# Four FFN products among the projection's last turns, half the stored tiles deferred in the merge, and a projection that opens with two tiles

## The chip, the cores and the metric

The kernel runs on one core of one Trainium2 chip. A core has TensorE (PE: matmuls, with a weight load of its own, PEld), VectorE (DVE), ScalarE (ACT), GpSimd (POOL), SyncE (SP) and 16 DMA engines that all queues share. Matmuls write to PSUM, eight banks of 512 fp32 columns for each partition. The metric is the device time of one execution in microseconds; less is better.

## The reference

One step of a hybrid backbone on 128 context and 1024 latent tokens, width 1024, fp32. Three token mixers (mLSTM, HGRN2, attention) give branches of width 512. What matters here is what follows them:

```
branches = jnp.stack([y_ml, y_hg, y_at], axis=2)
proj_b = jnp.einsum('blnw,nwd->blnd', branches, p['w_branch'])
gates_b = jax.nn.sigmoid(bg.reshape(B, L, N_BRANCH, D_MODEL))
merged = jnp.sum(gates_b * proj_b, axis=2)
x = x + g1 * (merged @ p['w_out'])

h2 = _rmsnorm(x, p['norm2_g']) * (1 + sc2) + sh2
gu = h2 @ p['w_ffn_in']
gt, up = gu[..., :FFN_HIDDEN], gu[..., FFN_HIDDEN:]
x = x + g2 * ((jax.nn.silu(gt) * up) @ p['w_ffn_out'])
```

FFN_HIDDEN is 2816, and a last RMSNorm gives the outputs.

## The kernel before

Every fp32 operand of a matmul is split in two parts (hi by ACT, a copy to fp32r; lo by DVE, the difference), and a product is three passes, hi*hi, hi*lo and lo*hi (`three_passes`, L59). Features lie on partitions and the 1152 tokens are columns (T = 1152, three groups of TH = 384), except where rows of tokens are needed. Each engine runs its own program, in the order written, and they meet by counting semaphores: `x.then_inc(s, 1)` on one, `wait_ge(s, n)` on another. Phases end with a barrier of all engines (L77 to L79).

**Merge** (`blend`, first half). For each of 8 tiles t of 128 output features, the sigmoid of three gate tiles multiplies three branch products, and the sum goes to `merged[:, t]`. The product of branch 0 was made earlier and lies in DRAM ("stored", `b0_dram`); branch 1 (operand `ys`, n=1) and branch 2 (operand `wide` in `zb`, n=2) are made here by `branch_tile`, 36 matmuls of 384 columns to three banks, 0 to 2 for even tiles and 3 to 5 for odd ones. The product n=1, t=0 is already in its banks when the phase begins. For n=1, DVE multiplies the stored tile by its gate into `merged` (L2300), takes the product out of PSUM times its gate to `part` (L2303) and adds it (L2307); for n=2 it does the last two (L2303, L2309). `taken` counts the operations that use up a gate, and PE starts a tile when the tile two before it has been taken. POOL issues the loads of gate tiles to a ring of four buffers (L2185), each when an older gate is used; SP issues stored tiles to two buffers (L2140), the parts of branch 2 (L2144), its weights (L2147) and w_out in eight parts (L2166). ACT makes the sigmoids (L2215). Between tiles ACT and DVE split branch 2 (L2275), its weights (L2279) and w_out (L2206, L2283), and at the end `merged` itself (`merged_hi` L2211, `merged_lo` L2289, which writes over the gate buffers).

**Projection** (`blend`, second half), nine tiles i of 128 tokens. PE: 48 matmuls of 512 columns, banks 2(i%2) and the next; then `turn(i-1)`, eight transposes (L2390). DVE: `residual` (times g1, L2336, count `gated`; plus x, L2340), `modulated` (two operations on the turned tile, L2348, L2351) and `split` (L2355). ACT: the store of x1 to DRAM (L2244), a square with sum (L2247), a scaling (L2251) and the hi part of the FFN's input (L2255). POOL: mean and power -0.5 (L2188, L2190). The FFN's first weight is split at the end (L2263, L2366).

**FFN** (`ffn`). 22 steps of 128 hidden features. In a step PE makes six products of 24 matmuls of 384 columns (gate for three token groups, then up), and puts 18 output products of the step before among them; step 0 has none and stands ahead of the loop. ACT makes silu (L2497), DVE multiplies by up (L2591), both split the result (L2501, L2596), and DVE adds each output product to `acc` (L2569), which takes the memory of `merged` and is loaded with x1 from DRAM (L2456).

## Time and profile before

| | us |
|---|---|
| median of 3 runs | 2532.36 |
| lowest, highest | 2531.53, 2533.96 |
| the profiled execution | 2528.88 |
| its span, first to last instruction | 2527.0 |
| merge, from the barrier ahead of it to PE's last product | 1449.97 to 1551.97 |
| projection, from PE's first matmul to its last turn | 1557.26 to 1673.45 |
| FFN, from PE's first matmul | 1682.52 on |

The span is what the rows add up to; the rest of an execution's time lies around it. The mean granted clock of TensorE is 0.985 of full speed; its two levels are 1.2 and 2.4 GHz (0.50 and 1.00). A row of the timeline gives the start, the busy time, the engine and line, and in brackets how long the engine stood idle before it and what released it. "issue" as a releaser means that the profile shows none. A stretch gives, for each engine, its busy time and its number of instructions, then the granted clock, the mean busy share of the DMA engines and what they moved.

### The profile page before, as it was taken

How to read it: one execution, taken by the hardware profiler on the slowest of the kernel's cores; microseconds unless marked ns; L12 is line 12 of the kernel's file. 1: busy time of each engine (PE TensorE's matmuls, PEld its weight loads, DVE VectorE, ACT ScalarE, POOL GpSimd, SP SyncE). 2: the span in 40 equal slices, each digit the busy share in tenths (PEclk: the TensorE clock that was granted, in tenths of full speed). 3: DMA queues.
4: the chain of work that ended last, by engine and by line, in shares of the span. 5: the costliest groups of instructions: out<-in, count | busy, mean ns of one | idle time of the engine just before them, and what ended most of it. 6: DMA issues, size and time to landing. Idle time of an engine off the chain costs nothing. (4 is left out here: it accounts for less than half of the span.)

```text
span 2527.0 us, 41706 instructions
## 1 busy us (share of the span) xinstructions
PE 2432.8 (96%) x17387; PEld 2240.3 (89%) x17387; DVE 1187.3 (47%) x1773; ACT 678.1 (27%) x1036; POOL 155.7 (6%) x194
## 2 busy tenths in 40 slices
PE   6999999999999999989999999979999999999998
PEld 4887789999999899888999898869999999999997
DVE  3331111003543667645555476445555555555555
ACT  3321111113332232234444453232112112112112
POOL 0000000001100011112111010110000000000000
PEclk8999999999999999999999999989999999999999
DMA  6224532225453333142002093231011011011012
GB/s 264 107 84 175 196 121 82 97 70 186 165 176 115 134 116 113 56 131 74 17 17 83 19 388 107 99 142 42 33 50 41 33 50 41 33 50 41 33 50 84
DMA packets 98125, 247.19 MB, mean 98 GB/s; under 512 B 12593, under 2 KB 56065, under 8 KB 88657
## 3 DMA queue, kind: packets, MB, share of 16 engines
q1 hardware_dynamic: 61200, 174.69, 20.0%
q10 hardware_dynamic: 32832, 55.46, 5.9%
q0 software_dynamic: 3968, 15.21, 1.6%
q8 instruction: 99, 1.62, 0.3%
q14 instruction: 26, 0.21, 0.0%
HBM read 183.85 MB, written 61.55 MB: 97 GB/s over the span
## 5 line engine op out<-in xcount | busy, mean ns | idle before, releaser
L59 PE MATMUL ps<-zb,wt 128*128 128x384 f32 x2400 | 651.5, 337 | 10.4 <-DVEq L2617 9.1
L59 PEld LDWEIGHTS ps<-zb,wt 128*128 128x128 f32 x2400 | 441.6, 188 | 28.4 <-DVEq L2617 9.5
L2569 DVE TENSOR_TENSOR merged<-merged,ps 128x512 f32<-128x512 f32 x378 | 259.5, 687 | 322.7 <-PE ps L59 320.1
L59 PE MATMUL ps<-xb,wt 128*128 128x384 f32 x1056 | 358.5, 340 | 0.0
L59 PE MATMUL ps<-ys 128*128 128x512 f32 x1056 | 298.2, 394 | 0.0
L59 PE MATMUL ps<-h_hi,fill_whi 128*128 128x384 f32 x672 | 234.7, 349 | 7.0 <-PEq L79 3.6
L59 PE MATMUL ps<-h_hi,fill_wlo 128*128 128x384 f32 x672 | 225.8, 336 | 0.0
L59 PE MATMUL ps<-h_lo,fill_whi 128*128 128x384 f32 x672 | 225.6, 336 | 0.0
L59 PEld LDWEIGHTS ps<-xb,wt 128*128 128x128 f32 x1056 | 198.5, 188 | 17.3
L59 PEld LDWEIGHTS ps<-ys 128*128 128x128 f32 x1056 | 193.3, 188 | 16.6
L59 PE MATMUL ps<-prj_whi,h_hi 128*128 128x512 f32 (+1 forms) x432 | 164.9, 382 | 6.1 <-DVE h_lo L553 6.1
L59 PE MATMUL ps<-prj_wlo,h_hi 128*128 128x512 f32 (+1 forms) x432 | 162.5, 376 | 0.0
L59 PE MATMUL ps<-prj_whi,h_lo 128*128 128x512 f32 (+1 forms) x432 | 162.3, 376 | 0.0
L1758 PEld LDWEIGHTS ps<-att_va,att_pt 128*128 128x128 f32 x1152 | 145.4, 191 | 6.6
L1758 PE MATMUL ps<-att_va,att_pt 128*128 128x65 f32 x1152 | 144.1, 270 | 0.0
L2501 ACT ACTIVATE ys<-zf 128x384 fp32r<-128x384 f32 x66 | 34.7, 526 | 395.8 <-DVE zf L2591 395.8
L538 DVE TENSOR_TENSOR prj_wlo<-prj_raw,prj_whi 128x2048 fp32r<-128x2048 f32 (+1 forms) x20 | 43.5, 2189 | 194.2 <-ACT prj_whi L454 193.9
L59 PEld LDWEIGHTS ps<-h_hi,fill_whi 128*128 128x128 f32 x672 | 126.6, 188 | 7.1 <-issue 4.2
L59 PEld LDWEIGHTS ps<-h_lo,fill_whi 128*128 128x128 f32 x672 | 127.0, 189 | 3.0 <-issue 3.0
L59 PE MATMUL ps<-h_hi,prj_whi 128*128 128x384 f32 x384 | 128.3, 334 | 0.8 <-ACT prj_tst L472 0.8
L59 PE MATMUL ps<-h_lo,prj_whi 128*128 128x384 f32 x384 | 128.3, 334 | 0.0
L59 PE MATMUL ps<-h_hi,prj_wlo 128*128 128x384 f32 x384 | 128.3, 334 | 0.0
(348 smaller groups left out, 3708.3 us busy)
## 6 DMA issues: line engine op xcount, KB each, us to landing
wraw<-in_w_ffn_in SPq DMA_DIRECT2D x22, 1024.0 KB, 4.8
prj_raw<-in_w_ada SPq DMA_DIRECT2D x16, 1024.0 KB, 5.9
fill_raw<-in_w_fill SPq DMA_DIRECT2D x30, 512.0 KB, 4.2
bg_dram<-fill_st ACTq DMA_DIRECT2D x72, 192.0 KB, 2.0
xf<-bg_dram POOLq DMA_DIRECT2D x24, 576.0 KB, 7.9
tok_dram<-prj_tst ACTq DMA_DIRECT2D x45, 256.0 KB, 2.1
zf<-in_w_ffn_out SPq DMA_DIRECT2D x22, 512.0 KB, 3.5
prj_raw<-in_w_tok SPq DMA_DIRECT2D x10, 1024.0 KB, 6.5
```

Source lines behind the costliest of these rows:

```text
L59: mm = pe.matmul(out, lhs[a], rhs[b], start=first and n == 0, stop=last and n == 2)
L538: v.tensor_tensor(w[1][b % 2][:, at], raw[u % NR][:, 0:width], w[0][b % 2][:, at].bitcast(F32), ALU.subtract).then_inc(lo_done, 1)
L1758: mm = pe.matmul(ps[:, OB, a * H1:a * H1 + H1], pt[j % 3][:, a * P:a * P + P], va[:, j, kv, :], start=False, stop=j == NT - 1 and a == G - 1)
L2501: act.activation(a[0][s][:, t * TH:t * TH + TH], gate[:, t * TH:t * TH + TH], ACT.Copy).then_inc(a_hi, 1)
L2569: v.tensor_tensor(dst, dst, ps[:, bank, :], ALU.add).then_inc(added, 1)
```

## The change

In the merge:

- The third tile (n=1, t=2) is written to banks 6, 7 and 2, and its first two thirds wait for nothing.
- Of the eight stored tiles, 4 to 7 are used in the second branch: their multiplication and addition stand ahead of the product of n=2, t=4 to 7. In n=1 these tiles have neither, and the product goes straight to `merged`. The order of the gate loads (`GATES`) follows, and `place` gives the count of each. SP loads both weights before stored tiles 4 and 5, and 6 and 7 after w_out.
- The first `merged_lo` stands between the last product and its addition. PE opens the projection when n=2, t=6 has been taken.

In the projection:

- Tiles 0 and 1 are multiplied together, part by part of the inner dimension.
- Turns lag by two tiles. Each x tile is loaded into the buffer where x1 is made, when the x1 of two tiles before has been stored and scaled, and DVE writes the product to `xs` first. The odd turned tiles go to `hole`.
- The FFN's first weight is split around tiles 2 and 3 into the free end of `merged` (`g.first_w`). After turn 7 PE makes the gate products of token groups 0 and 1, then turn 8, then their up products.

In the FFN: banks (2, 3, 6) for gate, (0, 1, 7) for up, 4 and 5 for output. PE makes only the third group of step 0, gate and up. ACT and DVE do the work of step 0 in a new order. SP waits for these two products before it loads the second half of x1, whose place `first_w` takes, and with it before the loop's loads.

```diff
@@ blend @@
+        APART = (6, 7, 2)
+        GATES = [(n, t) for t in range(4) for n in range(2)] + [(1, t) for t in range(4, 8)]
+        GATES += [(2, t) for t in range(4)] + [(n, t) for t in range(4, 8) for n in (0, 2)]
+        place = {x: i for i, x in enumerate(GATES)}
...
             for i in range(2, NT):
-                sp.wait_ge(x1_done, i - 1)
-                sp.dma_start(xin[i % 2], io["x_sample"][i * P - P:i * P, :]).then_inc(x_in[i % 2], 16)
+                sp.wait_ge(x_out[i % 2], 16 * (i // 2))
+                sp.wait_ge(xs_done, i - 1)
+                sp.dma_start(x1[i % 2], io["x_sample"][i * P - P:i * P, :]).then_inc(x_in[i % 2], 16)
...
+                        if n == 1:
+                            v.tensor_tensor(into, done[t % 2], bg[at % 4], ALU.mult).then_inc(taken, 1)
+                        else:
+                            link(v.tensor_tensor(done[t % 2], done[t % 2], bg[at % 4], ALU.mult))
+                            v.tensor_tensor(into, into, done[t % 2], ALU.add).then_inc(taken, 1)
...
+                    if n == 2 and t == 7:
+                        merged_lo(0)
...
+                if m == 2:
+                    branch_tile(pe, ps, t, [x[s] for x in w], ys[n], APART, range(2))
+                    pe.wait_ge(taken, place[1, 0] + 1)
+                    branch_tile(pe, ps, t, [x[s] for x in w], ys[n], APART, range(2, 3)).then_inc(mm_done, 1)
+                    continue
...
+            pe.wait_ge(taken, place[2, 6] + 1)
+            for k in range(KD):
+                pe.wait_ge(m_lo, k + 1)
+                pe.wait_ge(wo_lo, k + 1)
+                out(0, k)
+                if k == 0:
+                    pe.wait_ge(taken, 8 * NB)
+                out(1, k)
+            for i in range(2, NT):
+                pe.wait_ge(gated, i - 1)
+                for k in range(KD):
+                    out(i, k)
+                turn(i - 2)
...
+            turn(NT - 2)
+            pe.wait_ge(next_lo, 1)
+            pe.wait_ge(gated, NT - 1)
+            for t in range(2):
+                pe.wait_ge(h_lo, 3 * t + 3)
+                first(0, t)
             turn(NT - 1)
+            pe.wait_ge(gated, NT)
+            for t in range(2):
+                first(1, t)
@@ ffn @@
+            for n in range(2):
+                if n:
+                    sp.wait_ge(gu_mm, 6)
+                sp.dma_start(g.acc[:, 1 + 4 * n:5 + 4 * n, :],
+                             g.x1_dram[P + 4 * n * P:5 * P + 4 * n * P, :].rearrange("(t p) d -> p t d", p=P)).then_inc(x1_in[n], 16)
...
-            step(0, 0, first=True)
+            pe.sem_inc(gu_mm, 4)
+            for up in range(2):
+                for k in range(KD):
+                    mm = three_passes(pe, ps[:, (UP if up else GATE)[2], 0:TH], [x[:, k, up * P:up * P + P] for x in g.first_w],
+                                      [x[:, k, 2 * TH:3 * TH] for x in g.h], k == 0, k == KD - 1)
+                mm.then_inc(gu_mm, 1)
```

PE at the start of the merge, with the waits on `taken` (its semaphore is listed under the name of its first owner, prj_sig_done). Before:

```order
L59 MATMUL ps<-ys,wt 128x384 x36
L59 MATMUL ps<-ys,wt 128x384 [waits prj_sig_done]
L59 MATMUL ps<-ys,wt 128x384 x35
L59 MATMUL ps<-ys,wt 128x384 [waits prj_sig_done]
L59 MATMUL ps<-ys,wt 128x384 x35
```

The same place in the changed kernel:

```order
L59 MATMUL ps<-ys,wt 128x384 x60
L59 MATMUL ps<-ys,wt 128x384 [waits prj_sig_done]
L59 MATMUL ps<-ys,wt 128x384 x11
L59 MATMUL ps<-ys,wt 128x384 [waits prj_sig_done]
L59 MATMUL ps<-ys,wt 128x384 x35
```

The first wait now stands behind 60 matmuls instead of 36.

DVE at the end of the merge, n=2, from the product of t=6. In the kernel before L2303 is a product, L2309 its addition, L2283 a split of w_out and L2289 one of merged:

```order
L2303 TENSOR_TENSOR xf<-ps,xf 128x1152
L2309 TENSOR_TENSOR merged<-merged,xf 128x1152
L2283 TENSOR_TENSOR wt<-wraw,wt 128x1024
L2303 TENSOR_TENSOR xf<-ps,xf 128x1152
L2309 TENSOR_TENSOR merged<-merged,xf 128x1152
L2283 TENSOR_TENSOR wt<-wraw,wt 128x1024
L2289 TENSOR_TENSOR xb<-merged,zb 128x1152 x2
```

And in the changed one, where these are L2319, L2326, L2289 and L2295, and L2310 and L2311 use a stored tile:

```order
L2319 TENSOR_TENSOR xf<-ps,xf 128x1152
L2326 TENSOR_TENSOR merged<-merged,xf 128x1152
L2289 TENSOR_TENSOR wt<-wraw,wt 128x1024
L2310 TENSOR_TENSOR xf<-xf 128x1152
L2311 TENSOR_TENSOR merged<-merged,xf 128x1152
L2319 TENSOR_TENSOR xf<-ps,xf 128x1152
L2295 TENSOR_TENSOR xb<-merged,zb 128x1152
L2326 TENSOR_TENSOR merged<-merged,xf 128x1152
L2295 TENSOR_TENSOR xb<-merged,zb 128x1152
```

Two operations on the stored tile now stand ahead of the last product, and the first split of merged right behind it.

PE at the end of the projection, from the last matmul of tile 8. Before:

```order
L59 MATMUL ps<-wt,xb 128x512
L2390 MATMUL ps<-ident,merged 128x128 [waits prj_t_ev,prj_blk_done]
L2390 MATMUL ps<-ident,merged 128x128 x7
L2390 MATMUL ps<-ident,merged 128x128 [waits prj_t_ev,prj_blk_done]
L2390 MATMUL ps<-ident,merged 128x128 x7
L77 UNCONDITIONAL_BRANCH
L2677 UNCONDITIONAL_BRANCH [waits barrier_Pool_Activation_PE_DVE_SP_release]
L59 MATMUL ps<-zb,wt 128x384 [waits prj_rstd_done,fill_hi]
```

In the changed kernel (`mergedr` is the memory of `merged` under another type, here `first_w`):

```order
L59 MATMUL ps<-wt,xb 128x512
L2411 MATMUL ps<-ident,merged 128x128 [waits prj_t_ev,prj_blk_done]
L2411 MATMUL ps<-ident,merged 128x128 x7
L2411 MATMUL ps<-ident,merged 128x128 [waits prj_t_ev,prj_blk_done]
L2411 MATMUL ps<-ident,merged 128x128 x7
L59 MATMUL ps<-zb,mergedr 128x384 [waits prj_t_out0,prj_h_split,prj_t_out3]
L59 MATMUL ps<-xb,mergedr 128x384
L59 MATMUL ps<-zb,mergedr 128x384 x2
```

The two turns behind tile 8 are now 6 and 7, and FFN products follow them; turn 8 comes after 48 such matmuls and is followed by 48 more.

## Rows read from the trace of the kernel before

**Rows 1.** The page: busy time of PE and its share of the span.

```profile
PE 2432.8 (96%) x17387; PEld 2240.3 (89%) x17387; DVE 1187.3 (47%) x1773; ACT 678.1 (27%) x1036; POOL 155.7 (6%) x194
```

**Rows 2.** Waits of PE, 1440 to 1750 us: total, times, longest.

```profile
PE ps L59 <- DVEq L2617: 9.1, 1, 9.1
PE ps L2390 <- ACT merged L2251: 6.8, 1, 6.8
PE ps L59 <- issue: 6.7, 2, 5.3
PE ps L59 <- DVE xf L2303: 4.1, 1, 4.1
```

**Rows 3.** Stretches: length, busy time by engine, clock, DMA share, GB/s.

```profile
828.60:833.50 4.90, 4.87 (x128) 4.53 (x128) 0.34 (x2) 0.49 (x1) 0.00 (x0) 1.00 1.14 290
809.40:813.40 4.00, 4.00 (x14) 4.00 (x15) 1.21 (x1) 0.49 (x1) 0.58 (x2) 0.57 0.75 233
...
1456.46:1460.52 4.06, 0.00 (x0) 0.00 (x0) 2.73 (x3) 3.46 (x3) 0.54 (x1) 0.75 1.03 375
1460.52:1465.30 4.78, 4.78 (x15) 4.78 (x16) 4.71 (x4) 1.25 (x2) 1.56 (x3) 0.50 0.93 364
1465.30:1500.44 35.14, 35.14 (x203) 34.82 (x201) 27.18 (x21) 18.82 (x16) 5.46 (x11) 1.00 1.02 413
1502.00:1550.00 48.00, 48.00 (x278) 48.00 (x278) 30.89 (x23) 16.76 (x16) 3.24 (x6) 1.00 0.51 170
...
1557.26:1560.90 3.64, 3.64 (x9) 2.86 (x10) 3.64 (x4) 3.64 (x4) 0.00 (x0) 0.50 0.00 0
...
1581.90:1592.90 11.00, 11.00 (x51) 9.05 (x50) 4.23 (x4) 3.25 (x4) 1.32 (x2) 1.00 0.33 105
...
1673.45:1682.52 9.07, 0.00 (x0) 0.00 (x0) 6.06 (x5) 1.91 (x3) 0.28 (x1) 0.50 0.00 0
1682.52:1687.20 4.68, 4.68 (x15) 4.68 (x16) 0.00 (x0) 3.07 (x2) 0.71 (x2) 0.50 0.67 211
```

**Rows 4.** Timeline of DVE in the merge: the products of n=1, t=1, 2 and 3.

```profile
1463.17 1.35 DVE L2303 TENSOR_TENSOR xf<-ps,xf 128x1152 f32<-128x1152 f32 x1
...
1469.35 1.36 DVE L2303 TENSOR_TENSOR xf<-ps,xf 128x1152 f32<-128x1152 f32 x1 [1.47 <-PE ps L59]
...
1476.67 1.36 DVE L2303 TENSOR_TENSOR xf<-ps,xf 128x1152 f32<-128x1152 f32 x1 [1.51 <-ACT xf L2215]
```

**Rows 5.** Timeline of PE: three gaps and what released it.

```profile
809.38 0.41 PE L59 MATMUL ps<-h_hi,fill_whi 128*128 128x384 f32 x1 [2.11 <-PEq L79]
...
828.63 0.34 PE L59 MATMUL ps<-h_hi,fill_whi 128*128 128x384 f32 x1 [2.84 <-issue]
...
1449.97 6.49 PE L59 MATMUL ps<-ys,wt 128*128 128x384 f32 x36 [1.27 <-PEq L79]
```

**Rows 6.** Timeline of DVE at the end of the merge.

```profile
1552.01 1.36 DVE L2303 TENSOR_TENSOR xf<-ps,xf 128x1152 f32<-128x1152 f32 x1 [2.36 <-PE ps L59]
1553.40 1.36 DVE L2309 TENSOR_TENSOR merged<-merged,xf 128x1152 f32<-128x1152 f32 x1
1554.68 1.22 DVE L2283 TENSOR_TENSOR wt<-wraw,wt 128x1024 fp32r<-128x1024 f32 x1
1555.81 2.62 DVE L2289 TENSOR_TENSOR xb<-merged,zb 128x1152 fp32r<-128x1152 f32 x2
```

**Rows 7.** Timeline: residual of tile 8 on DVE, and its turn on PE.

```profile
1663.83 1.23 DVE L2336 TENSOR_TENSOR merged<-ps,zf 128x1024 f32<-128x1024 f32 x1 [5.78 <-PE ps L59]
...
1671.48 1.97 PE L2390 MATMUL ps<-ident,merged 128*128 128x128 f32 x8 [6.82 <-ACT merged L2251]
```

**Rows 8.** FFN opening: ACT's and DVE's weight splits; a load, us to landing.

```profile
1682.39 1.91 ACT L2491 ACTIVATE wt<-wraw 128x2048 fp32r<-128x2048 f32 x1 [2.41 <-SPq L2451]
...
1688.61 2.29 DVE L2563 TENSOR_TENSOR wt<-wraw,wt 128x2048 fp32r<-128x2048 f32 x1 [7.37 <-DMA hole<-gate_rows]
...
wraw<-in_w_ffn_in SPq DMA_DIRECT2D x1, 1024.0 KB, 11.4
```

More of the change, by code:

```diff
@@ L2081, in _, with branch_tile @@
             tile(7, False, False)
-def branch_tile(pe, ps, t, ws, y):
+def branch_tile(pe, ps, t, ws, y, banks=None, thirds=range(3)):
     ws = [x.rearrange("p (k n) -> p k n", k=4) for x in ws]
-    for c in range(3):
+    banks = banks or [3 * (t % 2) + c for c in range(3)]
+    for c in thirds:
         for k in range(4):
-            mm = three_passes(pe, ps[:, 3 * (t % 2) + c, 0:TH], [x[:, k, t % 4 * P:t % 4 * P + P] for x in ws],
+            mm = three_passes(pe, ps[:, banks[c], 0:TH], [x[:, k, t % 4 * P:t % 4 * P + P] for x in ws],
                               [y[:, 4 * b + k, c * TH:(c + 1) * TH] for b in range(2)], k == 0, k == 3)
     return mm
+GATE, UP, OUT = (2, 3, 6), (0, 1, 7), 4
 def blend(nc, g):
@@ L2260, in _ @@
                     split(i - 1)
-            act.wait_ge(ahead, 32)
-            act.wait_ge(o_mm, NT)
-            act.activation(g.wt[:, 0, :], raw[0], ACT.Copy).then_inc(next_hi, 1)
+                if i == 2:
+                    act.wait_ge(ahead, 32)
+                    act.activation(flat(g.first_w[0]), raw[0], ACT.Copy).then_inc(next_hi, 1)
             split(NT - 1)
@@ L2496, in gated @@
                     act.wait_ge(a_lo, 3 * j + t - 2)
-                act.activation(gate[:, t * TH:t * TH + TH], ps[:, GATE + t, 0:TH], ACT.Silu).then_inc(silu, 1)
+                act.activation(gate[:, t * TH:t * TH + TH], ps[:, GATE[t], 0:TH], ACT.Silu).then_inc(silu, 1)
             def a_split(j, s, t):
@@ L2528, in _ @@
             act.sem_inc(w_hi, 1)
-            step(0, 0, first=True)
+            w_split(1, 1, True)
+            for t in range(2):
+                gated(0, t, FIRST[0][t], True)
+            prompt_hi(0, 0, pw[0], True)
+            out_hi(0, 0, True)
+            a_split(0, 0, 0)
+            a_split(0, 0, 1)
+            gated(0, 2, FIRST[0][2], True)
+            a_split(0, 0, 2)
             with act.Fori(0, NH // 2 - 1) as i:
@@ L2596, in a_split, with step @@
                 v.tensor_tensor(a[1][s][:, r], gate[:, r], a[0][s][:, r].bitcast(F32), ALU.subtract).then_inc(a_lo, 1)
-            def step(j, s, first=False):
-                if not first:
-                    adds(j - 1, range(0, 3))
-                w_split(j + 1, 1 - s, first)
-                if not first:
-                    adds(j - 1, range(3, 6))
+            def step(j, s):
+                adds(j - 1, range(0, 3))
+                w_split(j + 1, 1 - s)
+                adds(j - 1, range(3, 6))
                 prompt_lo(j, s, pw[0], pw[1])
-                if not first:
-                    adds(j - 1, range(6, 9))
+                adds(j - 1, range(6, 9))
                 out_lo(j, s)
@@ L2609, in step @@
                     u = 9 + 3 * t
-                    if not first:
-                        adds(j - 1, range(u, u + 2))
+                    adds(j - 1, range(u, u + 2))
                     times_up(j, t, 3 + t)
-                    if not first:
-                        adds(j - 1, range(u + 2, u + 3))
+                    adds(j - 1, range(u + 2, u + 3))
                     a_split(j, s, t)
             v.sem_inc(w_lo, 1)
+            w_split(1, 1, True)
+            times_up(0, 0, FIRST[1][0])
+            times_up(0, 1, FIRST[1][1])
             v.wait_ge(g2_in, 32)
-            step(0, 0, first=True)
+            prompt_lo(0, 0, pw[0], pw[1])
+            out_lo(0, 0)
+            a_split(0, 0, 0)
+            a_split(0, 0, 1)
+            times_up(0, 2, FIRST[1][2])
+            a_split(0, 0, 2)
             v.wait_ge(cleared, 1)
-            v.wait_ge(x1_in, 32)
+            v.wait_ge(x1_in[0], 16)
             with v.Fori(0, NH // 2 - 1) as i:
@@ L2693, in group, with step @@
             def group(j, s, up, t, k):
[L2694 removed]
+                return three_passes(pe, ps[:, (UP if up else GATE)[t], 0:TH], [x[s][:, k, up * P:up * P + P] for x in w],
                                     [x[:, k, t * TH:t * TH + TH] for x in g.h], k == 0, k == KD - 1)
[L2697 removed]
+            def step(j, s):
                 pe.wait_ge(w_lo, j + 1)
@@ L2705, in step @@
                             mm.then_inc(gu_mm, 1)
-                        if k in (2, 5, 7) and not first:
+                        if k in (2, 5, 7):
                             u = 3 * n + (2, 5, 7).index(k)
                             out(j - 1, 1 - s, range(u, u + 1))
-            step(0, 0, first=True)
+            pe.sem_inc(gu_mm, 4)
[4 more added lines that the diff above has]
+                mm.then_inc(gu_mm, 1)
             with pe.Fori(0, NH // 2 - 1) as i:
@@ L2798, in build @@
         attention(nc, g)
-        g.merged = sb("merged", [P, KD, T])
+        with nc.sbuf_tensor("merged", [P, KD, T], F32) as g.merged:
+            pass
+        g.mergedr = sb("mergedr", [P, KD * T], F32R)
         with nc.sbuf_tensor("xf", [P, KD, T], F32) as g.xf:
```

124 lines of the change are left out of this document (59 added, 65 removed).

## Prediction

> **What bounds the kernel now.** I read the page first, then who waited for whom on TensorE (PE) between 1440 and 1750 us, then the stretches around each wait with their granted clock, then the rows of the engine that released PE. PE is busy for 96% of the span [rows 1], and no other engine is near that, so only two things can be won: time in which PE stands still, and time in which it works at its lower clock. Before the FFN's loop there are five standstills in the stages that the change touches [rows 2]: 4.07 us at the merge's third tile, 1.36 and 5.29 us (together the 6.7 of "issue", at 1500.44 and 1551.97), 6.82 us before the last turn and 9.07 us before the FFN. Behind three of them the clock is at half: 4.78 us at 0.50, 3.64 us at 0.50 and 4.68 us at 0.50 [rows 3]. All the rest of these 270 us is full-speed PE work, which the change neither adds nor removes: the same 144 products of the FFN's first step, the same 9 tiles, the same turns. The units are 35.14 us for 203 records, 0.173 us for a matmul of 384 columns (6.25 us for a merge tile of 36, 4.2 us for one FFN product of 24), and 11.00 us for a projection tile of 48; a turn adds 0.8 [rows 3].
>
> **The merge's opening.** Before, the third tile (t=2) starts at 1460.52, after VectorE (DVE) has taken the first tile out of its banks. After, two thirds of it (24 matmuls, 4.2 us) go to banks 6 and 7 and need no wait, so they run from 1456.3 to 1460.5; the last third then needs what is ready at 1460.5 anyway. PE reaches t=3 at 1462.6. That tile wants t=1 taken, which DVE ends at 1463.17 + 1.35 = 1464.5 [rows 4]: 1.9 us of new wait. t=3 ends at 1470.8. t=4 wants t=2 taken: 1469.35 + 1.36, now in two instructions, about 1470.9, no wait. It ends at 1477.1, and t=5 wants t=3 taken, at 1476.67 + 1.36 = 1478.0, because that product waited for its gate [rows 4]: 0.9 us. The gates of t=4 to 7 come one for each 6.25 us of PE instead of two; on the saturated queues (1.02 of the 16 engines, 413 GB/s, [rows 3]) they came some 2.9 us apart, so they are no bound. t=7 ends at 1484.3 + 2 x 6.25 = 1496.9, against 1500.44. The 1.36 us behind it also goes: DVE no longer makes the stored product and the addition in t=6 and can split the first weight half by 1494.3, since both weights are now loaded ahead of the deferred tiles. **Term A: 1501.81 - 1496.9 = 4.9 us.** Half of that is the half clock after the 4.07 us wait: 216 matmuls take 39.9 us before and 37.5 at full clock.
>
> **The merge's second half** has the deferred work: for t=4 to 7 DVE does four operations of 1.36 us instead of two, plus a split of 1.22 in two of the tiles, 6.7 us against PE's 6.25. Two of the four need no product of that tile and run while DVE waited before (it idled 2.36 us ahead of t=7 [rows 6]). Counted from t=3 with starts 1.28 us apart where nothing depends and 1.40 where it does, DVE reaches the last product 0.6 us after PE has ended it. PE itself is never held, since it needs a tile taken only two tiles later. **Term B, the seam to the projection.** Before: product 1.36, addition, one w_out split, then the first part of merged's lower half, which ends at 1557.2, and PE starts: 5.29 us [rows 6]. After: 0.6 late, product, then the lower half at once: 0.6 + 1.28 + 1.36 + 0.1 = 3.3 us. The gain is **2.0 us**. From there PE needs a new part only for each 12 matmuls (2.7 us) instead of each 6, and DVE delivers one every 1.3 to 2.6, so two tiles interleaved don't starve. The price of the clock behind this gap: 0 to 2.3 us. A gap of 2.84 us left it at 1.00, one of 2.11 us was followed by 4.00 us at a mean of 0.57, one of 4.06 us by half clock [rows 3, 5]. 3.3 lies nearer the last, so I take 1.8 (3.64 us at half clock costs 1.8, [rows 3]), as much as before, plus 0.3 us gained on the small waits inside the first tile. The Trainium skill ("TensorE: Matmul & The Clock Gate", What's actually happening) says that the number of matmuls at the low clock differs between runs of the same kernel; the rows above, where 2.11 us cost more than 2.84, agree, and by it this term is a draw of lots and not a rule of gap length.
>
> **Term C, the last turn.** Turns now lag by two tiles, and the residual of tile i waits for turn i-2. At the end PE does tile 8, turns 6 and 7 (1.6 us), then two FFN gate products (8.4), and only then turn 8. Counting from the end of tile 8, DVE first modulates tile 6 and splits tile 5 (0.9 to 4.6), then starts the residual of tile 8. From there to the turn it took 1671.48 - 1663.83 = 7.65 us before, by way of ScalarE's (ACT) square, GpSimd's power and ACT's scaling [rows 7]. So turn 8 can start at 12.25, and PE gets there at 10.0: a wait of 2.25 instead of 6.82, **4.6 us gained**. The products' own inputs are in time: split 5 at 4.6 against the second product at 5.8.
>
> **Term D, the barrier.** After turn 8 PE has two more products, 8.4 us, to 21.4. DVE does modulation 7, split 6, split 7 (ACT is free for it at 12.2), modulation 8 (needs turn 8, starts 14.5) and split 8, done at 19.3. So PE itself is last at the barrier, and the gap is what it was at the barrier ahead of the merge, which PE reached last as well, 1.27 us [rows 5], instead of 9.07: **7.8 us**. The weight split of 2.29 us has moved to tile 3, where DVE has 4 us to spare per tile. **Term E, the clock.** With no long gap there, the 4.68 us at half clock behind the barrier give 2.3 back, and the turn that took 1.97 us takes 0.8: **3.4 us** with rounding.
>
> **Term F, what is new in the FFN's opening.** PE has only two products (8.4 us) after the barrier before the second step, where before it had six (25 us). After 9 matmuls more, at 10.1, the first output product wants the first activation split (a_lo). The chain to that, from ACT's start [rows 8]: ACT's split 1.91, DVE's 2.29, but then the gate rows, which landed only at 1688.6, that is at 6.2; from there the lower half of 1024 columns at DVE's 1.23 us for as many [rows 7], two multiplications of 512 with the gate rows to 8.8, ACT's 1024 columns at 1.0 (half of its 1.91 for 2048), DVE's 1.23, and 0.6 for the 384 columns of the activation: 11.7. **Cost 1.6 us.** Before, this chain had 17 us of cover. A second one: SyncE now waits for those two products before it loads the second half of x1 (2 MB) and, behind that in its queue, the weight of step 2. DVE's split of that weight is queued ahead of its additions, and PE's sixth output product at 22.9 wants those. At 413 GB/s 3 MB take 7.6 us; landing at 17.5 to 18.5, then 1.9 + 2.3 + 0.7, gives 22.4 to 23.4: **0.3 us**. Another 0.1 for the third projection tile, which now waits for DVE to take the first.
>
> **The sum.** 4.9 + 2.0 + 0.3 + 4.6 + 7.8 + 3.4 - 1.6 - 0.3 - 0.1 = **21.0 us**. The profiled execution took 2528.9 us (span 2527.0), so the same one would be 2507.9. The median of the runs is 3.5 us higher, 2532.4, so I forecast 2511.4 us, 0.8% less. The bank numbers in the FFN's loop, the semaphore more and the buffer of the odd tiles cost nothing, because the loop is bound by PE and DVE idles beside it.
>
> **Rivals.**
> 1. The clock falls otherwise. If it stays up at the seam, 1.8 us less: 2509.6. If it also falls at one of the small waits (1.9, 2.25, 1.27, 1.6 us), 1.7 to 3.4 more: 2513 to 2515. For: the 2.11 us case [rows 5]. Against: the 1.36 us ahead of 1501.81 had 1.00 on both sides [rows 3].
> 2. The weight of step 2 comes late. For: the weight asked for at 1691 took 11.4 us to land behind the x1 loads [rows 8]. Landing at 21.4 instead of 18 costs 3.4 us: 2515. Against: 2 MB stood ahead of it then that are through now. The Trainium skill ("DMA: Bandwidth & Descriptors", Queues, rings and completion order) has each DMA engine take turns between its queues, a packet at a time; both loads are on one queue, so by that they come one after the other, as in my count.
> 3. The merge's second half is bound by DVE or by the gates, two of which are now needed per tile and are asked for only when older ones are used. If each of the last three tiles loses 1 to 1.5 us, 3 to 4.5 us: 2514 to 2516. Against: the second half moved 170 GB/s at 0.51 of the DMA engines [rows 3], and the four deferred tiles and gates add 4.7 MB, less than 100 GB/s, to it.
> 4. The change does not cover what it should: turn 7 stands ahead of the first FFN product, and its tile's chain ends at 12.25 after tile 7, while PE arrives at 12.6. If ACT or GpSimd is 3 us late there, the wait just moves ahead of the products, and the last turn's with it: up to 4 us, 2515.
> 5. Slower. The low clock, once there, holds on through the small waits: over the two seam tiles (20 us more) and from the end of tile 8 to the FFN's second step (29.2 us of full-speed work, less 3.9 of waits that it hides). That is 45 us more: 2557. It decides from 21 us of added time at half clock on. For: half clock held through the whole 9.07 us wait and 4.68 us beyond [rows 3]. Against: in the rows it was back after 3.6 to 4.8 us of work each time, and no gap over 3.3 us is left.
>
> **Chances.** Forecast (2509.5 to 2513) 0.60; clock stays up 0.10, falls again 0.08; late weight 0.08; second half 0.06; uncovered turn 0.03; no net gain 0.03; slower 0.02. A measurement of this kernel tells about 0.2%, 5 us, from no change, so faster 0.95, same 0.03, slower 0.02. The range takes in rivals 1 to 4 and one microsecond of spread of the median: 2506 to 2518.
>
> **What would show it.** PE's waits before the FFN's loop should read about 1.9, 0.9, 3.3, 2.3, 1.3 and 1.6 us. The second branch starts near 1496.9, the projection near 1550.4, and the clock is full from the projection's second tile on. The chain's last barrier is released by PE and not by DVE. Wrong would be: a wait of DVE for a stored tile or a gate beyond t=4, a wait at the first FFN products, half clock behind the barrier, or any PE wait inside the FFN's loop.

## The result and the profile after

| | before | after |
|---|---|---|
| median, us | 2532.82 (2531.53 to 2533.96, 4 runs) | 2512.17 (2509.91 to 2516.67, 4 runs) |
| ratio to before, 95% interval | | 0.9919, 0.9907 to 0.9931 |
| profiled execution, and its span | 2528.88, 2527.0 | 2512.39, 2510.5 |

The change takes 20.7 us off the median (by the interval 17.5 to 23.6). The forecast of 2511.4 us for the median was 0.8 us too low. The sum behind it, 2507.9 us for the profiled execution, was 4.5 us too low, and where these 4.5 us are is what most of the rest is about. All tables here count from S, PE's first matmul of the merge. The program ahead of S is the same in all kernels, but S lies anywhere from 1448.6 to 1456.2 us in the fourteen traces. In after it lies 1.4 us earlier than in before, so from S to the end the sum missed by 5.9 us and not by 4.5. Three executions of 4843, 5822 and 8446 us (one of before, two of `both_ends_again`), far outside all others, are left out of the ratios and of that kernel's median.

| us | merge, S to PE's last product | from there to PE's first matmul behind the FFN's barrier | from there to the end | S to the end |
|---|---|---|---|---|
| before | 102.0 | 130.6 | 844.5 | 1077.0 |
| forecast | 97.1 | 131.7 | 827.3 | 1056.0 |
| after | 97.2 | 132.6 | 832.1 | 1061.9 |
| the same kernel again | 96.0 | 131.6 | 831.8 | 1059.4 |

The forecast's row is that of before with the terms of the sum taken off, and 16.8 us (four products) moved from the third column into the second. The first two columns are right within 1.1 us. The third is 4.5 to 4.8 us off.

The page of after, its line of busy time, which answers to [rows 1]:

```profile
PE 2428.1 (97%) x17387; PEld 2233.9 (89%) x17387; DVE 1185.8 (47%) x1774; ACT 677.5 (27%) x1036; POOL 146.7 (6%) x194
```

The waits of PE in after, 1440 to 1750 us (total, times, longest), against [rows 2]:

```profile
PE ps L59 <- issue: 3.2, 1, 3.2
PE ps L59 <- DVE merged L2621: 3.0, 1, 3.0
PE ps L59 <- PEq L79: 2.4, 2, 1.2
PE ps L2411 <- ACT merged L2257: 2.1, 1, 2.1
PE ps L59 <- DVE xf L2319: 1.7, 1, 1.7
PE ps L59 <- DVE ys L2650: 1.5, 1, 1.5
PE ps L59 <- DVE xf L2317: 0.8, 1, 0.8
```

The 9.1, the 6.8 and the 4.1 are gone. The second line is new: PE waits 3.0 us for an addition of DVE in the FFN. The same waits in order of time, from the timeline of PE in after (start, busy, what; in brackets the wait and its releaser):

```profile
1448.58 13.02 PE L59 MATMUL ps<-ys,wt 128*128 128x384 f32 x72 [1.24 <-PEq L79]
1463.29 6.54 PE L59 MATMUL ps<-ys,wt 128*128 128x384 f32 x36 [1.70 <-DVE xf L2319]
1470.61 25.24 PE L59 MATMUL ps<-ys,wt 128*128 128x384 f32 x144 [0.78 <-DVE xf L2317]
1495.69 50.08 PE L59 MATMUL ps<-zb,wt 128*128 128x384 f32 x288
1548.96 1.19 PE L59 MATMUL ps<-ys,zb 128*128 128x512 f32 x2 [3.19 <-issue]
...
1667.75 1.09 PE L2411 MATMUL ps<-ident,merged 128*128 128x128 f32 x8 [2.07 <-ACT merged L2257]
...
1678.38 0.41 PE L59 MATMUL ps<-zb,mergedr 128*128 128x384 f32 x1 [1.18 <-PEq L79]
1690.05 0.95 PE L59 MATMUL ps<-wrawr,ys 128*128 128x512 f32 x3 [1.55 <-DVE ys L2650]
1703.62 0.97 PE L59 MATMUL ps<-ys 128*128 128x512 f32 x3 [2.95 <-DVE merged L2621]
```

The forecast was 1.9, 0.9, 3.3, 2.3, 1.3 and 1.6; the rows read 1.70, 0.78, 3.19, 2.07, 1.18 and 1.55. The fourth row is the whole second branch; it starts without a wait, 47.1 us behind S (forecast 46.9, before 51.8). The last row is the miss: 2.95 where the sum had 0.3.

Stretches of after (length, busy time by engine, granted clock, DMA share, GB/s), against [rows 3]:

```profile
1548.96:1554.60 5.64, 5.63 (x13) 4.43 (x14) 5.64 (x5) 5.64 (x7) 0.00 (x0) 0.50 0.00 0
...
1667.75:1677.20 9.45, 9.45 (x56) 9.13 (x56) 4.81 (x4) 1.96 (x2) 0.00 (x0) 1.00 0.01 2
1678.38:1688.50 10.12, 10.12 (x57) 9.80 (x57) 6.01 (x7) 6.47 (x7) 0.80 (x2) 1.00 0.90 306
...
1703.62:1707.10 3.48, 3.48 (x13) 3.34 (x14) 2.98 (x5) 0.00 (x0) 0.00 (x0) 0.67 0.83 294
```

The seam to the projection is followed by 5.64 us at half clock, where before had 3.64. That costs 2.8 us instead of 1.8, and is the 0.9 us by which the second column is off. Behind the last turn and behind the barrier the clock is full, as the forecast had it. Behind the new 2.95 us wait it stays full for 1.1 us and is then at half for 3.5 us.

What holds that wait is in the chain of waits of after, 1660 to 1712 us (start, us, what):

```profile
1678.38 8.57 PE ps L59 x48
...
1687.69 10.92 DMA wraw<-in_w_ffn_in
...
1698.73 1.93 ACT wt L2535
...
1702.89 0.69 DVE merged L2621
1703.58 0.04 issue
1703.62 8.58 PE ps L59 x35
```

PE's two products behind the barrier, then the load of step 2's weight, its split by ACT and, between the third and fourth row, by DVE, then the addition that was queued behind this split, then PE.

### The profile page after: what moved, and what is told of

Its sections match the earlier page's. It is cut to its first block and busy times, and to the rows that moved or that the text cites. A ratio compares the mean times of both kernels' runs of the same rounds, so it can differ in the third digit from the quotient of the medians.

```text
span 2510.5 us, 41707 instructions
## 1 busy us (share of the span) xinstructions
PE 2428.1 (97%) x17387; PEld 2233.9 (89%) x17387; DVE 1185.8 (47%) x1774; ACT 677.5 (27%) x1036; POOL 146.7 (6%) x194
## 5 line engine op out<-in xcount | busy, mean ns | idle before, releaser
L59 PE MATMUL ps<-zb,wt 128*128 128x384 f32 x2304 | 626.2, 336 | 0.0
L59 PEld LDWEIGHTS ps<-zb,wt 128*128 128x128 f32 x2304 | 423.5, 188 | 17.3
L59 PE MATMUL ps<-xb,wt 128*128 128x384 f32 x1008 | 342.0, 339 | 0.0
L59 PEld LDWEIGHTS ps<-xb,wt 128*128 128x128 f32 x1008 | 189.0, 187 | 17.3
```

The lines of the kernel that those rows point to most:

```text
L59: mm = pe.matmul(out, lhs[a], rhs[b], start=first and n == 0, stop=last and n == 2)
```

## Experiments

The kernels ran in three groups, each on a chip of its own, with the kernel before in each: `after_again`, `weight_first`, `both_ends` and `no_first` beside 2533.19 us, `split_early`, `no_first_wf`, `no_defer` and `no_apart` beside 2532.65, `one_tile`, `apart_alone`, `last_turn` and `both_ends_again` beside 2532.26. Ratios are to the kernel before of the same group. The changed kernel itself ran in the first group only.

### The changed kernel again

> The changed kernel once more, not altered. Its first trace had seven PE waits before the FFN's loop was under way: 1.70, 0.78, 3.19, 2.07, 1.18, 1.55 and 2.95 us, and half clock behind the seam (6.8 us) and behind the last of them (3.4 us). Theory 1 (waits come from the order of work, and only the clock is a draw): the seven waits come back within 0.3 us each, the time lies 18 to 23 us under the kernel before, and the runs spread by some 6 us with the granted clock. Theory 2 (the wait of 2.95 us is an accident of that execution): it is missing here, and the median is 3 us lower than 2512.

2512.47 us (2511.33 to 2518.2), ratio 0.9927 (0.9913 to 0.9941). Of the seven waits of the first trace four came back within 0.1 us. The 0.78 us in the merge is missing, the first output product waited 2.61 us instead of 1.55, with half clock behind it for 6.2 us, and at the addition behind the late weight PE waited only 0.33 us instead of 2.95. So neither theory held as it stood. The weight itself came no earlier: it took 12.2 us to land instead of 10.9, and PE was merely later. The FFN took 831.8 us against 832.1. So there are two bounds on one path, and what PE waits for at the first it doesn't wait for at the second.

### The weight of step 2 ahead, the splits ahead, and both

`weight_first` lets SP load step 2's weight before it waits for the two products and loads the second half of x1:

```diff
                 if n:
+                    load(2)
                     sp.wait_ge(gu_mm, 6)
...
-            with sp.Fori(0, NH - 2) as i:
-                load(i + 2)
-                load_out(i + 1)
+            load_out(1)
+            with sp.Fori(0, NH - 3) as i:
+                load(i + 3)
+                load_out(i + 2)
```

> SyncE loads the weight of FFN step 2 ahead of the second half of x1, and doesn't wait for the third group's products before it. Nothing else changes. Theory (the 2.95 us wait is DVE's weight split, queued ahead of its additions, which waits for a weight that lands 10.7 us after it is asked for): the weight lands by 8 us after the barrier, the 2.95 us wait is gone, and with it the half clock behind it: 3.0 us less than the changed kernel if the clock fell there seldom, 4.7 if always. Rival (the additions themselves, or the output products' other inputs, are late): the wait stays, at 2 us or more, and the time stays.

`split_early` has the two activation splits stand ahead of the output weight and its gate rows, here on DVE; on ACT they go ahead of `out_hi`:

```diff
+            a_split(0, 0, 0)
+            a_split(0, 0, 1)
             v.wait_ge(g2_in, 32)
             prompt_lo(0, 0, pw[0], pw[1])
             out_lo(0, 0)
-            a_split(0, 0, 0)
-            a_split(0, 0, 1)
```

> The changed kernel with the second half of both_ends alone: ACT and DVE split the first two activation groups ahead of the gate rows' work, while the weight of step 2 is still asked for after the third group's products. Theory 1 (the weight's landing is a bound of its own, counted from the barrier: in two traces PE got its sixth output product of step 1 at 25.2 and 26.5 us after the barrier, whatever it had waited before): the 1.55 to 2.6 us wait goes, the later one grows to 4 us or more, and the time is that of the changed kernel within 1.5 us. Theory 2 (the two waits add up): 1.5 to 2.5 us less, 2510.

`both_ends` has both.

> weight_first, and in FFN step 0 ACT and DVE also split the first two activation groups ahead of the gate rows' work (out_hi, prompt_lo), which waits for the gate rows. Theory: the first output product wants only p_lo and a_lo; a_lo then comes 5 us earlier, the 1.55 us wait of PE behind its first nine matmuls of step 1 falls to 0 to 0.2, since p_lo is ready 3 us earlier: 1.3 to 1.6 us less than weight_first. Rival (p_lo or the second weight part is as late): a wait of 1 us or more stays there, and nothing is gained.

> The changed kernel with weight and splits early once more, beside the kernel with the earlier last turn: 2506.5 to 2508.5, 5 us less than the changed kernel, if the first measurement holds; 2510 or above would mean that those 5 us were a draw of the clock.

| | median, us | ratio | FFN from the barrier on | S to the end |
|---|---|---|---|---|
| weight_first | 2511.76 (2511.1 to 2515.82) | 0.9918 (0.9904 to 0.9931) | 830.3 | 1059.6 |
| split_early | 2517.33 (2514.82 to 2521.66) | 0.9944 (0.993 to 0.9957) | 832.0 | 1059.7 |
| both_ends | 2507.49 (2504.57 to 2509.25) | 0.9901 (0.9886 to 0.9916) | 825.5 | 1053.3 |
| both_ends_again | 2508.3 (2504.63 to 2511.38) | 0.9907 (0.9892 to 0.9922) | 825.6 | 1055.2 |

The last row's median is of four executions. Timeline of PE in `weight_first`, then of DVE there, then of PE in `split_early`:

```profile
1696.26 1.64 PE L59 MATMUL ps<-wrawr,ys 128*128 128x512 f32 x3 [2.90 <-DVE ys L2652]
```

```profile
1690.76 1.23 DVE L2634 TENSOR_TENSOR wrawr<-zf,wrawr 128x1024 fp32r<-128x1024 f32 x1 [2.39 <-DMA hole<-gate_rows]
```

```profile
1695.13 0.97 PE L59 MATMUL ps<-ys 128*128 128x512 f32 x3 [0.30 <-DVE merged L2621]
1705.99 1.65 PE L59 MATMUL ps<-ys 128*128 128x512 f32 x3 [4.29 <-DVE merged L2621]
```

With the weight early, the second wait is gone and the first is there, 2.90 us, behind gate rows that DVE had to wait for. With the splits early, the first is gone (the 0.30 us is a new wait, for an addition to a later output product) and the second has grown to 4.29: PE arrives sooner at a point that stands 25.3 us behind the barrier, where after had it at 25.2. Either edit alone brings at most 2 us of the FFN in the trace. The time of `weight_first` is that of the changed kernel, not the 3.0 to 4.7 us less that was expected. The median of `split_early` lies some 4 to 6 us above the changed kernel's (by the ratios), though the two did not run in one group and its trace takes as long as after's from S on; that difference stays unexplained. Both edits together bring 6.3 to 6.6 us in the FFN against after, and 5.0 in the median beside the same kernel, 4.3 below `weight_first` where 1.3 to 1.6 were expected. Chain of waits of `both_ends`, then SP's queue there:

```profile
1678.97 0.19 issue
1679.16 32.98 PE ps L59 x176
```

```profile
1683.39 0.34 SPq L2487 DMA_DIRECT2D wraw<-in_w_ffn_in  x1
1687.75 0.37 SPq L2501 DMA_DIRECT2D merged<-x_dram  x1
```

The chain is PE alone now, 176 matmuls without a step to another engine. The weight is asked for 4.2 us behind the barrier instead of 9.3, and takes 10.8 us to land, against 10.9 in after and 12.2 in its second trace.

### The four products back behind the barrier

> The changed kernel, but all six products of FFN step 0 stand behind the barrier; merge, two opening tiles, lagging turns and first_w are as in the changed one. Theory (the four products are what covers the last turn's chain and DVE's tail): PE waits 9.5 to 10.6 us ahead of the last turn, 6 to 7 us at the barrier, and has 3 to 5 us of half clock behind it, while the waits of 1.55 and 2.95 us vanish: 8 to 12 us slower than the changed kernel, 2520 to 2524 us. Rival (the gain at the end comes from the lag of the turns alone): no more than 3 us slower.

`no_first` makes all six products of step 0 behind the barrier and keeps the rest of the change. `no_first_wf` does the same with the weight of step 2 early.

```diff
-            for t in range(2):
-                pe.wait_ge(h_lo, 3 * t + 3)
-                first(0, t)
             turn(NT - 1)
...
-            for up in range(2):
+            for up, t in ((0, 0), (0, 1), (1, 0), (1, 1), (0, 2), (1, 2)):
```

> no_first with weight_first in it: all six products of step 0 behind the barrier, and the weight of step 2 loaded ahead of the second half of x1, with no wait for these products. Theory (of the 19 us between no_first and the changed kernel, 4.5 us and the half clock behind it belong to the weight asked for 25 us late, the rest to the cover): the 4.5 us wait goes, 6 to 8 us less than no_first, 2523 to 2525. Rival (all of the 19 us is the cover): 2530 as no_first.

2531.26 us (2526.86 to 2535.37, 10 runs), ratio 0.9997 (0.9988 to 1.0006), and with the early weight 2525.68 (2523.65 to 2527.52, 7 runs), ratio 0.9973 (0.9962 to 0.9984). Timeline of PE in `no_first`:

```profile
1669.20 1.94 PE L2411 MATMUL ps<-ident,merged 128*128 128x128 f32 x8 [10.46 <-ACT merged L2257]
1677.13 0.66 PE L59 MATMUL ps<-zb,mergedr 128*128 128x384 f32 x1 [5.99 <-PEq L79]
...
1720.48 1.65 PE L59 MATMUL ps<-ys 128*128 128x512 f32 x3 [4.51 <-DVE merged L2614]
```

Without the products the lagged turns make the last one later than before (10.46 against 6.82 us), since other work of DVE now stands ahead of tile 8's residual; the barrier gives back 3.1 of it. And the weight of step 2 is late here too, behind six products, because SP waits for them: 4.51 us and half clock. That wait was not expected, and with it `no_first` is 19 us slower than the changed kernel beside it and not 8 to 12. The early weight removes it (FFN 844.0 instead of 850.8 us, before 844.5). So the rest of the change, which gains 5.5 us in the merge, pays nothing by itself while the weight is late, and 7 us once it is early. With both ends of the FFN's opening fed, the four products are worth 1069.2 - 1055.2 = 14.0 to 1069.2 - 1053.3 = 15.9 us from S on, and 17 to 18 us by the ratios. The terms C and D and the clock of E make 15.8.

### The merge: deferral and the third tile apart, one by one

> The changed kernel with all eight stored tiles used in the first branch, as before; gates and loads in the old order. The third tile still goes to banks 6, 7 and 2. Theory (the deferral is what lets DVE split branch 2's weight in time): PE ends the first branch as early as the changed kernel, or 0 to 2 us later where a gate or a stored tile is late, and then waits 3.5 to 5 us for the weight instead of 0, with half clock behind it; the seam's gap falls from 3.2 to 2.7. Together 4 to 7 us slower than the changed kernel, 2516 to 2519. Rival (DVE would be in time anyway): no slower than 1 us, or faster by the 0.5 us of the seam.

`no_defer` uses all eight stored tiles in the first branch, as before, and keeps the third tile in banks 6, 7 and 2. The loads of weights and stored tiles are back in the order of before.

```diff
-        GATES = [(n, t) for t in range(4) for n in range(2)] + [(1, t) for t in range(4, 8)]
-        GATES += [(2, t) for t in range(4)] + [(n, t) for t in range(4, 8) for n in (0, 2)]
+        GATES = [(n, t) for t in range(8) for n in range(2)] + [(2, t) for t in range(8)]
...
-                    if t < 4 if n == 1 else t >= 4:
+                    if n == 1:
```

> The changed kernel with the third merge tile in banks 0 to 2 again, in one piece, as before. Theory: the wait of 4.07 us comes back with about 2 us of half clock, and the waits of 1.70 and up to 0.78 us go: 3 to 4.5 us slower than the changed kernel, 2515.5 to 2517. Rival (the gates' arrival sets the pace of the first branch, and the early start only moves the wait): no more than 1 us slower.

`no_apart` keeps the deferral and puts the third tile back into banks 0 to 2:

```diff
-                if m == 2:
-                    branch_tile(pe, ps, t, [x[s] for x in w], ys[n], APART, range(2))
-                    pe.wait_ge(taken, place[1, 0] + 1)
-                    branch_tile(pe, ps, t, [x[s] for x in w], ys[n], APART, range(2, 3)).then_inc(mm_done, 1)
-                    continue
-                if m > 2:
+                if m >= 2:
```

`apart_alone` is the kernel before with the third tile in banks 6, 7 and 2.

> The kernel before with one part of the change alone: the third merge tile in banks 6, 7 and 2, two thirds of it ahead of the wait; all stored tiles are still used in the first branch. If parts add up, it takes away the 4.07 us wait and the half clock behind it: 3.5 to 4.9 us faster, 2528 to 2529. My theory is that they don't: the first branch ends 4 us sooner, but the weights of branch 2 still land behind eight stored tiles, as they did with deferral undone alone (4.31 us of wait for their split, against 1.36 in the kernel before). So a wait of 4 to 5 us appears before the second branch with half clock behind it, and nothing is left of the gain: 2531 to 2535.

| | merge, us | median, us | ratio |
|---|---|---|---|
| neither (before) | 102.0 | | |
| tile apart alone (apart_alone) | 103.8 | 2536.05 (2532.31 to 2539.05, 11 runs) | 1.0013 (1.0004 to 1.0021) |
| deferral alone (no_apart) | 99.8 | 2518.37 (2511.22 to 2522.41) | 0.9939 (0.9926 to 0.9953) |
| both (after, again, both_ends) | 97.2, 96.0, 96.4 | | |
| tile apart, rest of the change without deferral (no_defer) | 105.3 | 2523.89 (2518.02 to 2525.34) | 0.9957 (0.9943 to 0.9971) |

The other traces of kernels with both parts have 96.2 to 97.0 us. The tile apart makes things slower by itself (1.8 us in the merge, 1.0 to 5.3 us by the interval of the ratio) and gains 2.6 to 3.8 us of merge on top of the deferral. The deferral's own share, with the tile apart, is 8 to 9 us of merge; 4 to 7 us of time were expected, and by the ratios it is 8 to 10. Timelines of PE at the start of the second branch, in `no_defer` and in `apart_alone`:

```profile
1506.35 52.96 PE L59 MATMUL ps<-zb,wt 128*128 128x384 f32 x288 [4.31 <-DVE wt L2284]
```

```profile
1508.25 3.99 PE L59 MATMUL ps<-zb,wt 128*128 128x384 f32 x13 [3.74 <-DVE wt L2281]
```

The waits were 4.31 and 3.74 us, where before had 1.36; behind S these starts lie at 52.3 and 52.1 us, before at 51.8. What PE waits for is DVE's split of the weight. Timelines of DVE ahead of it, in before and then in `no_defer`:

```profile
1495.36 1.36 DVE L2300 TENSOR_TENSOR merged<-xf 128x1152 f32<-128x1152 f32 x1 [1.34 <-DMA xf<-b_dram]
...
1499.41 2.29 DVE L2279 TENSOR_TENSOR wt<-wraw,wt 128x2048 fp32r<-128x2048 f32 x1
```

```profile
1499.91 1.36 DVE L2307 TENSOR_TENSOR merged<-xf 128x1152 f32<-128x1152 f32 x1 [1.66 <-DMA xf<-b_dram]
...
1503.96 2.29 DVE L2284 TENSOR_TENSOR wt<-wraw,wt 128x2048 fp32r<-128x2048 f32 x1
```

The weight's own landing is not the bound: asked for at 1468.75, 1472.31 and 1475.15 us and landing 17.0 to 17.7 us later, it was there 36 us behind S in before, `no_defer` and `apart_alone` alike. The expectation of `apart_alone`, which puts the wait down to weights that land behind the stored tiles, had that wrong, and the prediction's reason that both weights are now loaded ahead of the deferred tiles was not needed. The split stands in DVE's program behind three operations of t=6, and the first of them waits for stored tile 6, which came 45.4 to 45.9 us behind S in all three, over DMA engines that are nearly full (shares 0.93 to 1.01 over 40 us). From there it is 6.4 to 6.7 us to PE's start. A wait taken away from PE ahead of that point comes back at it, with half clock behind. The deferral moves the point: it takes the stored tile out of t=6, and in after DVE, which now waits only for PE there, ends this split at 44.8 us behind S, and PE comes at 47.1. The split moved ahead of t=6's operations, with all stored tiles left in the first branch, was not run, so how much of the deferral's gain that alone would give is open.

### One tile at the projection's opening

```diff
                 out(0, k)
-                if k == 0:
-                    pe.wait_ge(taken, 8 * NB)
+            pe.wait_ge(taken, 8 * NB)
+            for k in range(KD):
                 out(1, k)
```

> The changed kernel, but the projection opens with one tile: all eight parts of tile 0, then the wait for the last product to be taken, then all eight parts of tile 1. My theory: the opening with two tiles hides the rate at which VectorE delivers the lower half of merged; with one tile TensorE wants a new part each 1.35 us at full clock while VectorE makes one each 1.3 us or more, so small waits of some tenths come back inside the first tile, which in the half-clock stretch cost nothing: 0.3 to 1.5 us more than the changed kernel, 2512.8 to 2514. The wait of 3.2 us ahead of it is the same. Rival: the two tiles matter for the seam's size, so that it grows to 4 us and more, 2515 or above; or they do nothing, 2512.3.

2517.72 us (2514.46 to 2519.13), ratio 0.9941 (0.9928 to 0.9954). Timeline of PE:

```profile
1551.89 1.19 PE L59 MATMUL ps<-ys,zb 128*128 128x512 f32 x2 [3.20 <-issue]
1556.79 0.74 PE L59 MATMUL ps<-ys,zb 128*128 128x512 f32 x2 [0.56 <-DVE xb L2295]
1559.19 0.73 PE L59 MATMUL ps<-ys,zb 128*128 128x512 f32 x2 [0.73 <-DVE xb L2295]
```

The seam is the same 3.2 us. Two waits for parts of `merged`, 1.3 us together, are back. The stage from the merge to the FFN is 1.8 to 2.8 us longer than in the two traces of after, but part of that is the clock: it fell behind the 2.07 us wait ahead of the last turn (3.4 us at a mean of 0.51, which costs 1.7 us), and was at half for a shorter time behind the seam. Without these the stage is about 1.5 us longer, the upper end of the 0.3 to 1.5 us expected. The 3.5 to 5.6 us in the median (by the ratios; another group) are more than that; where the rest would be, the trace doesn't show, and from S to the end (1060.2 us) it is as long as after.

### The residual of tile 8 ahead

```diff
                 residual(i)
+                if i == NT - 2:
+                    continue
+                if i == NT - 1:
+                    split(i - 3)
+                    modulated(i - 2)
```

The same on ACT: tile 8's square goes ahead of the split of tile 6. The rest is `both_ends`.

> The changed kernel with weight and splits early at the FFN's opening, and one thing more: behind the last projection tile VectorE does that tile's residual ahead of the split of tile 5 and the modulation of tile 6, and ScalarE the square ahead of its own part of them. My theory is that the 2.07 us wait before the turn of tile 8 is set by the chain that starts with this residual, which stood 3.7 us behind other work: it vanishes, and the second FFN product now wants its split at 5.8 us behind the tile, where it comes at 5.5 to 6.5, so 0 to 0.7 us of it come back. 1.4 to 2.1 us less than weight and splits early alone: about 2505.5 to 2506. Rival: the chain only moves, the second product waits 1.5 us or more, and the time is the same 2507.5.

2507.46 us (2502.31 to 2508.69), ratio 0.9903 (0.989 to 0.9916). Timelines of DVE and PE:

```profile
1654.79 1.23 DVE L2355 TENSOR_TENSOR merged<-ps,zf 128x1024 f32<-128x1024 f32 x1 [5.76 <-PE ps L2420]
```

```profile
1663.74 1.04 PE L2420 MATMUL ps<-ident,merged 128*128 128x128 f32 x8
```

The last turn comes 8.95 us behind the residual without waiting, and in its place PE waits only 0.18 us, for an addition in the FFN. The stage from the merge to the FFN takes 129.2 us, against 131.4 and 132.7 in the two traces of `both_ends`: 2.2 us or more, and from S to the end it is the shortest of all, 1051.3 us. The medians can't tell the two kernels apart, so the 1.4 to 2.1 us that were expected show in the trace alone.

## Why the prediction was right, and what it had wrong

**Term A, right.** 4.9 us against 4.8 in after's trace and 6.0 in the second. The wait of 0.9 us was named for t=5, because t=3's product would wait for its gate. It stands at t=4: the gate of t=2 came later (DVE waited 2.55 us for it), so t=2 was taken at 1470.56, and t=3 no longer waited long for its own. The size came out by luck, since the 0.9 us hung on when a gate came: of the nine other traces of kernels with both parts, one has 0.80 us there, and eight have 0.3 us or nothing. The term exists only as a pair: the tile apart alone gives less than nothing. The prediction had the 1.36 us wait go by the deferral, but did not say that without it the early tile is worth nothing.

**Term B, right.** DVE reaches the last product 0.5 us after PE has ended it (0.6 forecast). From the timeline of DVE in after, against [rows 6]:

```profile
1546.25 1.35 DVE L2319 TENSOR_TENSOR xf<-ps,xf 128x1152 f32<-128x1152 f32 x1
1547.52 1.35 DVE L2295 TENSOR_TENSOR xb<-merged,zb 128x1152 fp32r<-128x1152 f32 x1
```

The seam was 3.19 or 3.20 us in eleven traces, and each time the clock was at half behind it, at once or within 1 us, for 3 to 6 us; that cost 1.5 to 3.1 us where the sum had 1.8. Rival 1's first half (it stays up, 1.8 us less) didn't happen once. By the Trainium skill ("TensorE: Matmul & The Clock Gate", What's actually happening) the number of matmuls at the low clock differs between runs of one kernel; that it falls at all after 3.19 us was no draw in these traces.

**Terms C and D, right.** From the residual of tile 8 to its turn, after has 1660.10 to 1667.75, the 7.65 us of before. The turn waited 2.07 (2.25), the barrier 1.18 (1.27), and no half clock follows in after: **term E** held in this trace. The 2.07 us gap is followed by half clock in one trace of nine (`one_tile`).

**Term F, the step that failed.** The term that was mis-sized is the second wait of the FFN's opening, for the weight of step 2, with 0.3 us. "3 MB take 7.6 us; landing at 17.5 to 18.5". The weight landed at 1698.62 - 1678.38 = 20.2. It was asked for at 9.3 and not at 8.4, since the x1 half goes out ahead of it. From then to the landing the stretch moved more than 3 MB, at less than 413 GB/s:

```profile
1678.38:1687.69 9.31, 9.31 (x54) 9.31 (x55) 5.74 (x6) 5.66 (x6) 0.80 (x2) 1.00 0.89 297
1687.69:1698.62 10.93, 9.38 (x50) 8.53 (x49) 5.16 (x8) 2.23 (x5) 0.00 (x0) 1.00 0.93 370
```

370 x 10.93 is 4.0 MB: besides the 3.1 MB that I counted, some 0.4 MB of the 3.1 MB asked for right behind the barrier (in its 9.31 us only 2.8 MB moved), and part of the next output weight, asked for 1.9 us after. From landing to PE it took 5.0 us (4.9 forecast). So the wait was 2.95 us instead of 0.3, and behind it came half clock that cost 1.7 us, which the sum had not at all: 4.4 of the 4.8 us in the FFN's column; the other 0.4 us show as no wait. Rival 2, held at 0.08, is what happened in this trace, with 2.65 us of wait more than in the sum where it priced 3.4, and with half clock that it didn't price. What was said against it, that what stood ahead would be through, the first of these two rows refutes for the 0.4 MB.

The second trace loses 4.1 of its 4.5 us elsewhere on the same path: 1.0 us more at the first output product (2.61 instead of 1.6) and 3.1 us of half clock behind that, which is the second half of rival 1 (it falls at one of the small waits too). There the weight wait is 0.33 us as in the sum, but not for the sum's reason: the weight landed at 21.5 us, even later, and PE was slowed ahead of it. That the late weight is a bound of its own is shown by `split_early` (4.29 us) and `both_ends` (neither wait).

The Trainium skill ("DMA: Bandwidth & Descriptors", Queues, rings and completion order) has the descriptors of one queue taken in order on each DMA engine; with the output weight landing 1.2 us behind the weight of step 2, though both were under way together, the trace agrees. That rule gives the order. It gives no time, and the time was the error.

The wait for the first activation split (a_lo) was forecast as 1.6 and read 1.55, but it is a draw: it follows the landing of the second load of gate rows, which differs from execution to execution with the same loads ahead of it.

| | no_apart | after | one_tile | after_again | no_defer | weight_first |
|---|---|---|---|---|---|---|
| gate rows, us to landing | 5.2 | 5.4 | 5.6 | 6.5 | 6.6 | 6.8 |
| a_lo wait, us | 1.35 | 1.55 | 1.79 | 2.61 | 2.69 | 2.90 |

My chain was right in structure, with 5.4 us for the landing as in before; other traces show up to 1.4 us more.

**Why the median came out all the same.** I added 3.5 us to go from the profiled execution to the median, because before's lay that much below its own. After's profiled execution lies 0.2 us above its median. So the miss of 4.5 us and this step of 3.5 nearly cancel, and the 4.5 itself would have been 5.9 had S not lain 1.4 us earlier. That the median was hit within 0.8 us is luck. That it lies within 2506 to 2518 is not: a miss of 5.9 us would still have left it there. From S on the traces give a gain of 15.1 and 17.6 us, the forecast was 21.0, and the medians say 20.7 with an interval that begins at 17.5. One profile of before is too little to say which of these is nearer; S alone differs by 7.6 us among traces of the same code.

**The other rivals.** 3 did not happen: the second half of the merge never held PE. 4 neither: PE has no wait at turn 7 or the first products. 5 neither: half clock was over within 6.2 us of work each time.

## What to carry to other kernels

A wait on the path can hide a second bound just behind it, which is set by loads and stands at a time of its own, not at a distance from the wait; ask for each wait that you take away when the next engine's data will be there at the earliest, and move that too. Here the tile apart without the deferral cost 1.0 to 5.3 us, and each of two edits at the FFN's opening gave nothing in the median where both gave 5. When work moves from behind a barrier to ahead of it, what followed it loses its cover: count the bytes that stand in the queues at that moment, all of them, and ask for the next weight ahead of bulk that is needed later.

## What the runs showed of the hardware

- Behind waits of 2.6 us and more in these stages the clock was at half every time, at once or within 2 us: eleven seams of 3.19 or 3.20 us, one of 2.76, eleven others from 2.61 to 4.51 us, and the longer ones. It stayed there for 3 to 6 us of work. Behind the twelve waits of about 1.7 us in the merge it never was, and behind nine of 2.07 once. It is no rule of the gap's length alone: in [rows 3, 5], elsewhere in the kernel before, it fell behind 2.11 us and stayed at 1.00 behind 2.84.
- A load of 256 KB of gate rows, asked for at the same place of the same queue, took 5.2 to 6.8 us in fourteen traces.
- The load of 1 MB for step 2's weight took 9.9 to 12.2 us in these traces: 10.8 when asked for 4.2 us behind the barrier (`both_ends`), 10.9 and 12.2 when asked for 9.3 us behind it (after and its second trace), with the DMA engines at a share of 0.93 and 0.86 in the last two.
